# A hybrid decoder step: no drains in the product loops, four banks for the output products, and a sample recurrence on VectorE and ScalarE alone

## The chip, the cores and the metric

One core of one Trainium2 chip runs the whole program. The metric is the device time of one execution in microseconds. The kernel before was run three times: 4519.31 us in the median, 4514.93 to 4529.73 us.

## What is computed

One inference step of one layer of a hybrid decoder, for a prompt of 1024 tokens and for 8 samples of 4 tokens (1056 tokens together, D = 1024, everything float32). Only the token mixer is touched by the change:

```
proj = RMSNorm(h) @ w_in        # gates (3 D) | RWKV-7 (3328) | S5 (1024) | Mamba-2 (z, xBC, dt)
o_r, o_s, o_m = RWKV-7, S5, Mamba-2 of their columns, each projected to D
merged = sig(g_r)*o_r + sig(g_s)*o_s + sig(g_m)*o_m
```

The RWKV-7 state of a sample is, for each of 16 heads, a 64 x 64 matrix S (value x key). For each of the 4 tokens:

```
sa = S a                                        # one number per value row
S  = S diag(w) + sa b^T + v k^T
y  = S r
```

S5 also needs, per channel group, a small Toeplitz kernel made from products of two coefficient tables. After the mixer come cross-attention and a squared-ReLU MLP.

## The kernel before

Every large product is made of three float32r passes: a weight tile is split into a high part (a rounding copy on ScalarE) and a low part (a subtraction on VectorE), and so is the input; TensorE adds hi*hi, hi*lo and lo*hi in PSUM. The 1056 tokens are three column chunks of 352. A block is 128 output columns: 8 contraction tiles x 3 passes x 3 chunks = 72 matmuls.

The order on each engine is written out by hand. Each stage is a set of generators, one per engine and kind of work, that yield a nominal time before they issue something; `weave` merges the generators of an engine by that time. Each engine then works through its own queue in that order, and semaphores join them. A wait therefore holds up all that stands behind it on its engine.

- `Columns` (L143 to L224) makes the input projections in three runs (weights named pz, pa and pb in the trace), 91 blocks, with the S5 and Mamba-2 work woven between. The high copy of the weights of block b (`high`, L188) overwrites a buffer that block b-2 read. TensorE says that it has been read with a drain at the end of each block (L213).
- `S5Input` (L265 to L349) makes the S5 input in two halves, with the same kind of drain, eight times (L347).
- `S5Weights` (L528 to L631) makes the S5 Toeplitz kernels, in 8 rounds. In each, two times eight products (L600), contraction 64, 16 output rows and 128 columns, go to the same 16 partitions of bank 5; the second half waits until ScalarE has moved the first out (L619).
- `Sums` (L1590 to L1763) makes the output products of the branches: 32 jobs of one block each, nominally 13 us apart. Jobs 0 to 7 and 8 to 15 are moved out of PSUM by ScalarE (L1734; the second eight with a sigmoid), jobs 16 to 31 by VectorE (L1754), which also combines every job from 8 on with its gate (L1763). VectorE makes the low part of the weights (L1683) one block ahead, and, at jobs 0, 8, 16 and 24, that of a new input (L1701), in chunks. The chunks go in turn to two PSUM banks, 6 and 7. Each job ends with a drain (L1721), for which `high` (L1677) waits.
- `RwkvSamples` (L1769 to L2053) is woven into the same stage. It builds the six vectors r, w, k, v, a, b of the 32 sample tokens, sends them through DRAM so that a partition holds one sample and head (128 of them), and then runs the recurrence: state, `tmp` and `sw` are tiles of 64 x 64 per partition in `sum_region`. VectorE works in four parts of 128 x 1024: state times a (L1982), its sums (L1986), sa b^T (L1990), plus `sw` (L1996), plus `sw` again (L2003), times r (L2008), its sums (L2012). `sw` is made by GpSimd in one instruction each, first the decayed state (L2050), then v k^T (L2053). VectorE waits for each, and GpSimd waits for VectorE to have read the one before. The first token waits for the vectors (`v_in`) and the state to land.
- `Tails` (L2056 to L2112) transposes the last tokens for some of the outputs, in the same stage, with banks 5 and 0.

The high copy of the sums before is:

```
act.wait_ge(self.loaded[b % 2], 16 * (b // 2 + 1))
if b >= 2:
    act.wait_ge(self.used, b - 1)
self.nc.scalar.activation(self.hi[:, b % 2, :, :], self.raw[:, b % 2, :, :], ACT.Copy).then_inc(self.w_hi, 1)
```

## Time and profile before

| | us |
|---|---|
| median of three runs | 4519.31 |
| the profiled execution, its own time | 4515.67 |
| its span | 4513.9 |
| TensorE busy | 4102.0 |
| VectorE busy | 2517.0 |
| ScalarE busy | 1420.3 |
| GpSimd busy | 222.7 |
| projections with S5 and Mamba-2 | 264 to 1843 |
| branch sums with the sample recurrence | 1860 to 2366 |
| prompt RWKV-7, then attention and MLP | from 2370 on |

Times of the trace count from the start of the span. A row in time gives start, length, engine and line; in brackets is the idle time ahead of it and what ended it. Matmuls overlap, so the distance between two starts says how fast they flow, not the length. Rows of waits give the total, how often and the longest.

### The profile page before, as it was taken

To read this page: it belongs to the slowest core of one execution; us is meant where nothing else is said; L and a number is where in the kernel's file an instruction comes from. 1 tells how busy PE (TensorE), PEld (TensorE's weight loads), DVE (VectorE), ACT (ScalarE), POOL (GpSimd) and SP (SyncE) were. 2 spreads that over 40 slices of the span, in tenths; PEclk is the share of its full clock that TensorE was granted. 3 is DMA by queue.
4 is the path that set the end of the run, shared out by engine and by line. 5 is a ranking of instruction groups with operands and counts; after the bars stand their busy time and mean duration, and the time that the engine had idled before them with its cause. 6 is when DMAs were issued, how large, how long until landed. Compare 5 with 4: busy or idle time off the path is not lost. (4 is left out here: it accounts for less than half of the span.)

```text
span 4513.9 us, 84409 instructions
## 1 busy us (share of the span) xinstructions
PE 4102.0 (91%) x35797; PEld 3747.0 (83%) x35797; DVE 2517.0 (56%) x4994; ACT 1420.3 (31%) x2428; POOL 222.7 (5%) x161
## 2 busy tenths in 40 slices
PE   8789999989989999878886999987998899999998
PEld 4779989989978888777885777776977889999997
DVE  3334646431278885258766877765553255444446
ACT  2112222221167553322103444433531252111112
POOL 0000000000001111022110000000001100000000
PEclk9899999989989999988997999998999999999999
DMA  5222222233355554545541100005222221111112
GB/s 186 77 84 83 89 82 88 69 98 112 104 146 142 159 145 123 155 141 163 176 141 40 32 29 31 32 13 174 92 96 89 74 90 61 47 47 47 39 37 77
DMA packets 374261, 418.68 MB, mean 93 GB/s; under 512 B 49162, under 2 KB 315964, under 8 KB 373020
## 3 DMA queue, kind: packets, MB, share of 16 engines
q1 hardware_dynamic: 361599, 368.01, 26.8%
q0 software_dynamic: 7680, 27.97, 2.1%
q10 hardware_dynamic: 4608, 17.30, 1.0%
q8 instruction: 285, 4.67, 0.4%
q14 instruction: 89, 0.73, 0.1%
HBM read 289.10 MB, written 121.77 MB: 91 GB/s over the span
## 5 line engine op out<-in xcount | busy, mean ns | idle before, releaser
L1718 PE MATMUL bank<-sum_x_hi,sum_w_hi 128*128 128x352 f32 x768 | 262.8, 342 | 95.4 <-DVE sum_x_lo L1701 38.0
L210 PE MATMUL bank<-xn_hi,pz_whi 128*128 128x352 f32 (+1 forms) x984 | 328.2, 334 | 21.0 <-DVE pz_wlo L195 14.9
L210 PE MATMUL bank<-xn_hi,pz_wlo 128*128 128x352 f32 (+1 forms) x984 | 319.7, 325 | 0.0
L210 PE MATMUL bank<-xn_lo,pz_whi 128*128 128x352 f32 (+1 forms) x984 | 318.0, 323 | 0.0
L3071 PE MATMUL bank<-bx_hi,bp_whi 128*128 128x384 f32 (+1 forms) x768 | 273.8, 357 | 29.7 <-DVE bx_lo L3129 18.4
L224 ACT ACTIVATE ring<-bank 128x352 f32<-128x352 f32 (+1 forms) x273 | 125.6, 461 | 536.0 <-PE bank L210 535.6
L210 PE MATMUL bank<-xn_hi,pb_whi 128*128 128x352 f32 x816 | 274.9, 337 | 18.9 <-DVE pb_wlo L195 13.0
L210 PE MATMUL bank<-xn_lo,pb_whi 128*128 128x352 f32 x816 | 266.1, 326 | 0.0
L210 PE MATMUL bank<-xn_hi,pb_wlo 128*128 128x352 f32 x816 | 265.2, 325 | 0.0
L1718 PE MATMUL bank<-sum_x_lo,sum_w_hi 128*128 128x352 f32 x768 | 256.5, 334 | 0.0
L1718 PE MATMUL bank<-sum_x_hi,sum_w_lo 128*128 128x352 f32 x768 | 256.3, 334 | 0.0
L3692 PE MATMUL bank<-bx_hi,bp_whi 128*128 128x384 f32 (+1 forms) x768 | 251.2, 327 | 4.7 <-issue 4.7
L3692 PE MATMUL bank<-ml_hidden_hi,bp_whi 128*128 128x384 f32 (+1 forms) x768 | 254.5, 331 | 0.0
L3071 PE MATMUL bank<-bx_lo,bp_whi 128*128 128x384 f32 (+1 forms) x768 | 253.1, 330 | 0.0
L3071 PE MATMUL bank<-bx_hi,bp_wlo 128*128 128x384 f32 (+1 forms) x768 | 253.0, 329 | 0.0
L3692 PE MATMUL bank<-bx_lo,bp_whi 128*128 128x384 f32 (+1 forms) x768 | 248.6, 324 | 0.0
L3692 PE MATMUL bank<-bx_hi,bp_wlo 128*128 128x384 f32 (+1 forms) x768 | 248.1, 323 | 0.0
L3692 PE MATMUL bank<-ml_hidden_hi,bp_wlo 128*128 128x384 f32 (+1 forms) x768 | 247.8, 323 | 0.0
L3692 PE MATMUL bank<-ml_hidden_lo,bp_whi 128*128 128x384 f32 (+1 forms) x768 | 247.6, 322 | 0.0
L1718 PEld LDWEIGHTS bank<-sum_x_hi,sum_w_hi 128*128 128x128 f32 x768 | 152.6, 199 | 105.6 <-issue 75.9
L3055 DVE TENSOR_TENSOR bp_wlo<-ring,bp_whi 128x512 fp32r<-128x512 f32 x192 | 131.4, 688 | 156.1 <-ACT bp_whi L3049 154.9
L3667 ACT ACTIVATE bp_whi<-ring 128x512 fp32r<-128x512 f32 x152 | 92.0, 627 | 394.4 <-PE bank L3692 391.4
(695 smaller groups left out, 12227.7 us busy)
## 6 DMA issues: line engine op xcount, KB each, us to landing
ring<-in_w_in_dram SPq DMA_DIRECT2D x90, 512.0 KB, 4.9
proj_scratch<-ring SPq DMA_DIRECT2D x66, 528.0 KB, 3.0
m_seg<-acum_scratch SPq DMA_DIRECT2D x32, 512.0 KB, 7.0
ring<-in_mlp_w_dram SPq DMA_DIRECT2D x16, 1024.0 KB, 5.6
ring<-in_mlp_w_dram SPq DMA_DIRECT2D x32, 512.0 KB, 3.5
gates_scratch<-ring SPq DMA_DIRECT2D x24, 528.0 KB, 4.7
merged_scratch<-sum_gate ACTq DMA_DIRECT2D x24, 528.0 KB, 5.7
m_raw<-proj_scratch SPq DMA_DIRECT2D x24, 512.0 KB, 5.5
```

Of the source, the lines that this page charges most:

```text
L210: last = self.nc.tensor.matmul(ps[0:n, 0:m], w[:, q, 0:n], self.pair[x][:, q, t0:t0 + m], start=q == 0 and j == 0, stop=q == KD - 1 and j ...
L224: self.nc.scalar.activation(self.staging[0:n, b % 2, t0:t0 + m], self.banks[e % len(self.banks)][0:n, 0:m], func).then_inc(self.off, 1)
L1718: last = self.nc.tensor.matmul(self.banks[e % n][:, 0:m], w[:, b % 2, q, :], self.pair[x][:, q, t0:t0 + m], start=q == 0 and i == 0, stop= ...
L3055: self.nc.vector.tensor_tensor(self.lo[:, hu % 4, :, :], raw, self.hi[:, hu % 4, :, :], ALU.subtract).then_inc(self.w_lo, 1)
L3071: last = self.nc.tensor.matmul(ps, w[:, hu % 4, q, :], self.pair[x][:, 4 * hf + q, t0:t0 + m], start=hf == 0 and q == 0 and i == 0, stop=h ...
L3667: self.nc.scalar.activation(self.pr.hi[:, hv % 4, :, :], self.raw(hv), ACT.Copy).then_inc(self.w_hi, 1)
L3692: last = self.nc.tensor.matmul(ps, w[:, s, q % 4, :], x[h][:, q, t0:t0 + m], start=q == 0 and j == 0, stop=q == 4 * v.halves - 1 and j == 2)
```

## The change

Five edits. (1) The drains of `Columns` and `Sums` are gone; the high copy waits for the counter of finished chunks instead. (2) In `S5Input` each drain becomes a signal of the matmul itself. (3) The two halves of the S5 kernel products go to partitions 0 to 15 and 64 to 79 of the bank, alternate, and no longer wait for a copy between them. (4) `Sums` gets banks 4 to 7; the samples and `Tails` move to banks 0 to 3, and one sum of the samples also waits for `sig`, whose reader has to be through with bank 1. (5) GpSimd's part of the recurrence is gone: VectorE multiplies the state with w in place, and ScalarE makes v k^T with 64 instructions per token, each a copy of k (128 x 64) scaled by one v per partition.

```diff
@@ Columns.high; Sums.high has the same edit @@
             if b >= 2:
-                act.wait_ge(self.used, b - 1)
+                act.wait_ge(self.product, 3 * (b - 1))
@@ Columns.multiply; Sums.multiply has the same edit @@
                 last.then_inc(self.product, 1)
-            pe.drain().then_inc(self.used, 1)
@@ S5Input.scalar @@
-                if s:
+                if s and q < KD - 1:
                     act.wait_ge(self.freed, q + 1)
+                elif s:
+                    act.wait_ge(self.product, Q5 + 1)
@@ S5Input.tensor @@
-                    if i == Q5 and s == 0:
-                        pe.drain().then_inc(self.freed, 1)
+                    if i == Q5 and s == 0 and q < KD - 1:
+                        last.then_inc(self.freed, 1)
@@ S5 kernel products @@
-            for half in range(2):
-                yield self.at(z, -0.40 + 0.05 * half)
-                pe.wait_ge(self.made_c, z + 1)
-                pe.wait_ge(self.off, 2 * z + 2)
-                if half:
-                    pe.wait_ge(self.kern_off, 2 * z + 1)
-                at = slice(64 * half, 64 * half + 64)
-                for q in range(QP):
-                    for ri in range(2):
-                        last = nc.tensor.matmul(bank[0:GC, q * P:(q + 1) * P], v.bb[at, ri, q0 + q, :],
+            yield self.at(z, -0.40)
+            pe.wait_ge(self.made_c, z + 1)
+            pe.wait_ge(self.off, 2 * z + 2)
+            for q in range(QP):
+                for ri in range(2):
+                    for half in range(2):
+                        at = slice(64 * half, 64 * half + 64)
+                        last = nc.tensor.matmul(bank[64 * half:64 * half + GC, q * P:(q + 1) * P], v.bb[at, ri, q0 + q, :],
...
-                last.then_inc(self.turned, 1)
+            last.then_inc(self.turned, 2)
@@ RwkvSamples.tensor @@
         pe.wait_ge(self.k_sq, 1)
-        nc.tensor.matmul(bank[3][:, 0:W], k.ones64[:, :], flat(T[5]), start=True, stop=True).then_inc(self.k_sum, 1)
+        pe.wait_ge(self.sig, 1)
+        nc.tensor.matmul(bank[1][:, 0:W], k.ones64[:, :], flat(T[5]), start=True, stop=True).then_inc(self.k_sum, 1)
@@ RwkvSamples.scalar @@
+        for t in range(TS):
+            for i in range(64):
+                yield self.RECUR - 2 + t * self.TOKEN + 0.5 * i
+                if t == 0 and i == 0:
+                    act.wait_ge(self.v_in, 16 * NB)
+                if t and i == 0:
+                    act.wait_ge(self.vk_used, t)
+                last = activation(self.sw[:, i, :], self.vt[:, t, RX_K, :], ACT.Copy, scale=self.vt[:, t, RX_V, i:i + 1])
+            last.then_inc(self.vk_made, 1)
@@ RwkvSamples.vector @@
             for i, h in enumerate(part):
                 yield at + 18 + 1.5 * i
-                if i == 0:
-                    dve.wait_ge(self.sw_made, t + 1)
                 dve.drain()
-                last = tt(st[:, h, :], tmp[:, h, :], sw[:, h, :], ALU.add)
-            last.then_inc(self.sw_used, 1)
+                tt(st[:, h, :], st[:, h, :], row(t, RX_W), ALU.mult)
+            for i, h in enumerate(part):
+                yield at + 24 + 1.5 * i
+                dve.drain()
+                tt(st[:, h, :], tmp[:, h, :], st[:, h, :], ALU.add)
@@ RwkvSamples.pool, removed whole @@
-            pool.tensor_tensor(sw, st, row(t, RX_W), ALU.mult).then_inc(self.sw_made, 1)
-            yield at + 24
-            pool.wait_ge(self.sw_used, t + 1)
-            pool.tensor_tensor(sw, vt[:, t, RX_V, :].unsqueeze(2).broadcast_to([P, N, N]), row(t, RX_K), ALU.mult).then_inc(self.vk_made, 1)
@@ branch_sums @@
-        sums = Sums(k, ctx, "sum", pair, inputs, jobs, k.bank[6:8], 13.0)
+        sums = Sums(k, ctx, "sum", pair, inputs, jobs, k.bank[4:8], 13.0)
```

ScalarE's queue where the recurrence starts. L1677 is now L1676, L1693 is L1692, L1734 is L1732, the store L1666 is L1665, and L1910 is a new row of v k^T. Before:

```order
L1734 ACTIVATE sum_gate<-bank7 128x352
L1734 ACTIVATE sum_gate<-bank6 128x352
L1666 DMA merged_scratch<-sum_gate 128x1056
L1677 ACTIVATE sum_w_hi<-ring 128x1024
L1693 ACTIVATE sum_x_hi<-ring 128x8x352
L1734 ACTIVATE sum_gate<-bank7 128x352
L1693 ACTIVATE sum_x_hi<-ring 128x8x352
```

And now:

```order
L1732 ACTIVATE sum_gate<-bank7 128x352
L1910 ACTIVATE sum_region<-sum_region 128x64 x3
L1732 ACTIVATE sum_gate<-bank4 128x352
L1910 ACTIVATE sum_region<-sum_region 128x64 x2
L1665 DMA merged_scratch<-sum_gate 128x1056
L1910 ACTIVATE sum_region<-sum_region 128x64 x2
L1676 ACTIVATE sum_w_hi<-ring 128x1024
L1910 ACTIVATE sum_region<-sum_region 128x64 x5
L1692 ACTIVATE sum_x_hi<-ring 128x8x352
L1732 ACTIVATE sum_gate<-bank5 128x352
L1910 ACTIVATE sum_region<-sum_region 128x64 x8
L1692 ACTIVATE sum_x_hi<-ring 128x8x352
```

The first of the new rows, with its wait for `v_in`, stands ahead of the last copy out of job 6, of all of job 7's, and of the high parts of job 8's weights and input.

VectorE's queue in the middle of the first token. Before:

```order
L1996 TENSOR_TENSOR sum_region<-sum_region 128x1024 x4
L1683 TENSOR_TENSOR sum_w_lo<-ring,sum_w_hi 128x1024
L1763 TENSOR_TENSOR sum_gate<-sum_gate,sum_prev 128x1056
L2003 TENSOR_TENSOR sum_region<-sum_region 128x1024 x4
L1683 TENSOR_TENSOR sum_w_lo<-ring,sum_w_hi 128x1024
```

And now, with L1682 for L1683 and L1761 for L1763:

```order
L2002 TENSOR_TENSOR sum_region<-sum_region 128x1024 x4
L2006 TENSOR_TENSOR sum_region<-sum_region 128x1024 x4
L1682 TENSOR_TENSOR sum_w_lo<-ring,sum_w_hi 128x1024
L1761 TENSOR_TENSOR sum_gate<-sum_gate,sum_prev 128x1056
L2012 TENSOR_TENSOR sum_region<-sum_region 128x1024 x4
L1682 TENSOR_TENSOR sum_w_lo<-ring,sum_w_hi 128x1024
```

The decay (L2002) is four instructions more ahead of the same low part of the weights; the rest keeps its place.

## Rows read from the trace of the kernel before

**Rows 1.** The page: busy time, share of the span and count of instructions, by engine.

```profile
PE 4102.0 (91%) x35797; PEld 3747.0 (83%) x35797; DVE 2517.0 (56%) x4994; ACT 1420.3 (31%) x2428; POOL 222.7 (5%) x161
```

**Rows 2.** Stretches: length, busy time of five engines, granted clock, DMA share, GB/s.

```profile
264.00:927.00 663.00, 640.99 (x4782) 594.19 (x4782) 338.98 (x1058) 166.94 (x292) 0.00 (x0) 1.00 0.27 82
1975.00:2366.00 391.00, 314.26 (x1793) 304.11 (x1791) 300.50 (x221) 60.84 (x64) 71.78 (x18) 0.90 0.47 153
```

**Rows 3.** TensorE in time (start, length): end of a projection block.

```profile
603.16 0.32 PE L210 MATMUL bank<-xn_hi,pz_wlo 128*128 128x352 f32 x1
603.74 0.40 PE L210 MATMUL bank<-xn_hi,pz_whi 128*128 128x352 f32 x1 [0.26 <-issue]
```

**Rows 4.** TensorE in time: between two column chunks of one block.

```profile
1880.45 0.32 PE L1718 MATMUL bank<-sum_x_hi,sum_w_lo 128*128 128x352 f32 x1
1880.61 0.32 PE L1718 MATMUL bank<-sum_x_hi,sum_w_hi 128*128 128x352 f32 x1
```

**Rows 5.** Drains in TensorE's queue: count, ns min/median/max, first and last start.

```profile
L213 PEldq DRAIN  x91: 3062/3088/3125, 274.1 to 1839.0; - x91
L1721 PEldq DRAIN  x32: 3050/3050/4558, 1873.4 to 2358.8; - x32
L347 PEldq DRAIN  x8: 843/860/4010, 184.4 to 194.2; - x8
```

**Rows 6.** TensorE in time: row-tiled products, then the S5 kernel products.

```profile
648.02 0.71 PE L739 MATMUL bank<-s_ca,s_H 64*128 64x128 f32 x8 [0.26 <-issue]
...
658.79 1.90 PE L600 MATMUL bank<-s_ca,s_bb 64*16 64x128 f32 x16 [0.78 <-ACT s_wb L613]
```

**Rows 7.** TensorE's waits from 1975 to 2366 us: total, times, longest.

```profile
PE bank L1718 <- DVE sum_prev L1754: 29.0, 7, 12.6
PE bank L1718 <- DVE sum_x_lo L1701: 17.4, 1, 17.4
PE bank L1718 <- ACT sum_gate L1734: 13.2, 6, 3.1
PE bank L1718 <- DVE sum_gate L1754: 10.2, 3, 9.7
```

**Rows 8.** GpSimd in time, one of its eight products.

```profile
2036.67 9.95 POOL L2050 TENSOR_TENSOR sum_region<-sum_region 128x4096 f32<-128x4096 f32 x1 [6.41 <-DVE sum_region L2003]
```

**Rows 9.** VectorE in time: one row beside that product, one free of it.

```profile
2037.82 9.93 DVE L1763 TENSOR_TENSOR sum_gate<-sum_gate,sum_prev 128x1056 f32<-128x1056 f32 x1
...
2059.36 1.26 DVE L1763 TENSOR_TENSOR sum_gate<-sum_gate,sum_prev 128x1056 f32<-128x1056 f32 x1
```

**Rows 10.** GpSimd's products by group: busy, mean ns, idle before.

```profile
L2050 POOL TENSOR_TENSOR sum_region<-sum_region 128x4096 f32<-128x4096 f32 x4 | 37.5, 9364 | 47.4 <-DVE sum_region L2003 35.1 <-DMA sum_region<-vec_scratch 12.3
L2053 POOL TENSOR_TENSOR sum_region<-sum_region 128x4096 f32<-128x4096 f32 x4 | 29.2, 7294 | 207.9 <-DVE sum_region L1996 207.9
```

**Rows 11.** VectorE by group, 1981 to 2325 us.

```profile
L1763 DVE TENSOR_TENSOR sum_gate<-sum_gate,sum_prev 128x1056 f32<-128x1056 f32 x20 | 47.4, 2371 | 1.7
L2008 DVE TENSOR_TENSOR sum_region<-sum_region 128x1024 f32<-128x1024 f32 x16 | 36.4, 2278 | 1.3
L1982 DVE TENSOR_TENSOR sum_region<-sum_region 128x1024 f32<-128x1024 f32 x16 | 28.2, 1765 | 23.6 <-DMA sum_region<-vec_scratch 22.1 <-issue 0.4
L1996 DVE TENSOR_TENSOR sum_region<-sum_region 128x1024 f32<-128x1024 f32 x16 | 19.6, 1226 | 1.3
```

**Rows 12.** In time around the recurrence's start: VectorE, then TensorE.

```profile
1981.49 11.16 DVE L1982 TENSOR_TENSOR sum_region<-sum_region 128x1024 f32<-128x1024 f32 x2 [22.05 <-DMA sum_region<-vec_scratch]
...
1998.21 0.63 PE L1718 MATMUL bank<-sum_x_hi,sum_w_hi 128*128 128x352 f32 x1 [17.43 <-DVE sum_x_lo L1701]
1998.64 0.49 PE L1718 MATMUL bank<-sum_x_lo,sum_w_hi 128*128 128x352 f32 x1
1998.94 0.49 PE L1718 MATMUL bank<-sum_x_hi,sum_w_lo 128*128 128x352 f32 x1
```

**Rows 13.** ScalarE by group: the nearest to the new rows.

```profile
L1443 ACT ACTIVATE r_U<-bank 128x64 f32<-128x64 f32 x128 | 28.5, 222 | 98.5 <-PE bank L1086 98.5
```

More of the change, by code:

```diff
@@ L618, in scalar @@
                     act.wait_ge(self.placed[1 - s], 16 * Q5 * ((z + 1) // 2))
-                activation(v.kern[:, half:ZG:2, :], bank[0:GC, :].rearrange("p (q n) -> p q n", q=QP), ACT.Copy).then_inc(self.kern_off, 1)
+                activation(v.kern[:, half:ZG:2, :], bank[64 * half:64 * half + GC, :].rearrange("p (q n) -> p q n", q=QP), ACT.Copy).then_inc(self.kern_off, 1)
     def sync(self, sp, used):
@@ L1598, in __init__ @@
         self.loaded, self.stored, self.gate_in, self.prev_in, self.x_in = two("loaded"), three("stored"), three("gate_in"), three("prev_in"), two("x_in")
-        self.w_hi, self.w_lo, self.used, self.product, self.done, self.x_hi, self.x_lo, self.sig = (
-            S("w_hi"), S("w_lo"), S("used"), S("product"), S("done"), S("x_hi"), S("x_lo"), S("sig"))
+        self.w_hi, self.w_lo, self.product, self.done, self.x_hi, self.x_lo, self.sig = (
+            S("w_hi"), S("w_lo"), S("product"), S("done"), S("x_hi"), S("x_lo"), S("sig"))
         self.off = [S(f"off{i}") for i in range(len(banks))]
@@ L1675, in high @@
             if b >= 2:
-                act.wait_ge(self.used, b - 1)
+                act.wait_ge(self.product, 3 * (b - 1))
             self.nc.scalar.activation(self.hi[:, b % 2, :, :], self.raw[:, b % 2, :, :], ACT.Copy).then_inc(self.w_hi, 1)
@@ L1720, in multiply @@
                 last.then_inc(self.product, 1)
-            pe.drain().then_inc(self.used, 1)
     def evacuate_scalar(self, act):
@@ L1851, in tensor @@
         pe.wait_ge(self.k_sq, 1)
-        nc.tensor.matmul(bank[3][:, 0:W], k.ones64[:, :], flat(T[5]), start=True, stop=True).then_inc(self.k_sum, 1)
+        pe.wait_ge(self.sig, 1)
+        nc.tensor.matmul(bank[1][:, 0:W], k.ones64[:, :], flat(T[5]), start=True, stop=True).then_inc(self.k_sum, 1)
         yield 44
         pe.wait_ge(self.bon, 1)
-        nc.tensor.matmul(bank[4][:, 0:W], k.ones64[:, :], flat(T[6]), start=True, stop=True).then_inc(self.bon_sum, 1)
+        nc.tensor.matmul(bank[2][:, 0:W], k.ones64[:, :], flat(T[6]), start=True, stop=True).then_inc(self.bon_sum, 1)
         six = [self.pm[:, 0:8, :], T[0], T[7], self.pm[:, 16:24, :], T[9], T[8]]
@@ L1864, in tensor @@
             for q in range(4):
-                last = nc.tensor.transpose(bank[(5, 0)[n % 2]][0:NS, q * P:(q + 1) * P], six[n // 2][:, 4 * (n % 2) + q, :], k.ident[:, :])
+                last = nc.tensor.transpose(bank[(3, 0)[n % 2]][0:NS, q * P:(q + 1) * P], six[n // 2][:, 4 * (n % 2) + q, :], k.ident[:, :])
             last.then_inc(self.tok_turned, 1)
@@ L1880, in tensor @@
         pe.wait_ge(self.squared, 1)
-        nc.tensor.matmul(bank[4][:, 0:W], k.ones64[:, :], self.f0, start=True, stop=True).then_inc(self.varsum, 1)
+        nc.tensor.matmul(bank[0][:, 0:W], k.ones64[:, :], self.f0, start=True, stop=True).then_inc(self.varsum, 1)
     def scalar(self, act):
@@ L1910, in scalar @@
         act.wait_ge(self.varsum, 1)
-        activation(self.f1, k.bank[4][:, 0:W], ACT.Ln, bias=k.eps[:, 2:3], scale=1.0 / 64)
+        activation(self.f1, k.bank[0][:, 0:W], ACT.Ln, bias=k.eps[:, 2:3], scale=1.0 / 64)
         act.drain()
@@ L1960, in vector @@
         dve.wait_ge(self.bon_sum, 1)
-        tt(self.bonus, bank[4][:, 0:W].rearrange("p (j t) -> p j t", t=NS), val, ALU.mult).then_inc(self.bonused, 1)
+        tt(self.bonus, bank[2][:, 0:W].rearrange("p (j t) -> p j t", t=NS), val, ALU.mult).then_inc(self.bonused, 1)
         for n in range(12):
@@ L1966, in vector @@
                 dve.wait_ge(self.tails.out, 16 * (3 + NB))
-            nc.vector.tensor_copy(self.tok[:, (n // 2) * D + (n % 2) * 512:(n // 2) * D + (n % 2 + 1) * 512], bank[(5, 0)[n % 2]][0:NS, :]).then_inc(self.tok_off, 1)
+            nc.vector.tensor_copy(self.tok[:, (n // 2) * D + (n % 2) * 512:(n // 2) * D + (n % 2 + 1) * 512], bank[(3, 0)[n % 2]][0:NS, :]).then_inc(self.tok_off, 1)
         N = 64
@@ L2003, in vector @@
                 last = tt(st[:, h, :], st[:, h, :], sw[:, h, :], ALU.add)
-            last.then_inc(self.st_made, 1)
+            last.then_inc(self.vk_used, 1)
             for i, h in enumerate(part):
@@ L2036, in vector @@
         tt(y, y, bank[2][:, 0:W], ALU.mult).then_inc(self.gated, 1)
-    def pool(self, pool):
-        N = 64
-        st, sw, vt = self.st, self.sw, self.vt
-        row = lambda t, a: vt[:, t, a, :].unsqueeze(1).broadcast_to([P, N, N])
-        for t in range(TS):
-            at = self.RECUR + t * self.TOKEN
-            yield at
-            if t == 0:
-                pool.wait_ge(self.v_in, 16 * NB)
-                pool.wait_ge(self.s_in, 16)
-            else:
-                pool.wait_ge(self.st_made, t)
-            pool.tensor_tensor(sw, st, row(t, RX_W), ALU.mult).then_inc(self.sw_made, 1)
-            yield at + 24
-            pool.wait_ge(self.sw_used, t + 1)
-            pool.tensor_tensor(sw, vt[:, t, RX_V, :].unsqueeze(2).broadcast_to([P, N, N]), row(t, RX_K), ALU.mult).then_inc(self.vk_made, 1)
 class Tails:
@@ L2101, in tensor @@
             for q in range(n):
-                last = self.nc.tensor.transpose(self.k.bank[(5, 0)[i % 2]][0:TAIL, q * P:(q + 1) * P], self.tile[:, a + q, :], self.k.ident[:, :])
+                last = self.nc.tensor.transpose(self.k.bank[(3, 0)[i % 2]][0:TAIL, q * P:(q + 1) * P], self.tile[:, a + q, :], self.k.ident[:, :])
             last.then_inc(self.turned, 1)
@@ L2111, in vector @@
             c = a if a < RT else a - RT
-            self.nc.vector.tensor_copy(self.rows[:, c * P:(c + n) * P], self.k.bank[(5, 0)[i % 2]][0:TAIL, 0:n * P]).then_inc(self.copied, 1)
+            self.nc.vector.tensor_copy(self.rows[:, c * P:(c + n) * P], self.k.bank[(3, 0)[i % 2]][0:TAIL, 0:n * P]).then_inc(self.copied, 1)
 def branch_sums(k, v):
@@ L2140, in _ @@
             def _(pool):
-                weave(later(samples.sync(pool), late), later(samples.pool(pool), late), tails.sync(pool))
+                weave(later(samples.sync(pool), late), tails.sync(pool))
             @block.tensor
```

8 lines of the change are left out of this document (4 added, 4 removed).

## The prediction

> **What bounds it now.** The page first: TensorE is busy 91% of the span, GpSimd 5% [rows 1]. Then the stretches [rows 2]: in the first projection run TensorE works 641 of 663 us at full clock, so what ends there is TensorE's own stream; in the part of the branch sums where the recurrence runs it works 314 of 391 us at a mean granted clock of 0.90, and VectorE is busy for 300.5. So two things are to be read: what breaks TensorE's stream where it is full, and whom it waits for in the sums.
>
> TensorE in time answers the first. Two matmuls of 352 columns start 0.16 us apart, also across a chunk that has a satisfied wait [rows 4]; across a block's end the distance is 0.58 us, with 0.26 us idle that nothing but "issue" ends [rows 3]. What stands there alone is the drain, of which there are 91, 32 and 8 [rows 5]. A drain row is 3.1 us long, but that is the time the queue runs ahead of the array; the array loses 0.58 - 0.16 = 0.42 us.
>
> The waits answer the second. From 1975 us on TensorE waits 29.0 + 10.2 us for VectorE to empty a bank, 13.2 for ScalarE to do so and 17.4 for the new input's low part [rows 7]. Behind them stands GpSimd: while one of its products runs for 9.95 us, a VectorE instruction that takes 1.26 us alone takes 9.93 [rows 8, 9]. It is not slowed by a share, it stands still until GpSimd is done. GpSimd's eight products sum to 66.7 us [rows 10], and on three lines of VectorE the excess over the undisturbed row is 22 (L1763: 47.4 - 20 x 1.26), 17 (L2008) and 9 us (L1982, both against 19.6) [rows 9, 11]: 48 us found, at most 66.7.
>
> **Part by part.**
>
> *Drains of the projections.* 91 x 0.42 would be 38 us. Where the next work is a small product of S5 or Mamba-2 the array would have paused a little anyway, so I count 0.34 on average: 31 us. Bounds: nothing, if another engine is just behind TensorE everywhere, and 38. I stay near the upper end, because 641 of 663 us busy leaves no room for another gate [rows 2].
>
> *Drains of S5Input.* Eight, at most 0.42 each [rows 3, 5]; I take 2 us of 0 to 3. The signals of single matmuls that replace seven of them cost nothing: matmuls with a signal stand at each chunk's end and the next starts 0.16 us later [rows 4].
>
> *S5 kernels.* Sixteen products take 1.90 us one after the other; eight of the same contraction and columns, on two row groups in turn, take 0.71 us with their fill [rows 6]. Without the last product's own length (some 0.27 of it) that is 0.10 us against 0.055 us each. 16 x 0.05 x 8 rounds is 6 us, and one entry fewer in some rounds another: 7 us. Bounds 0 (the halves do not overlap) and 9.
>
> *Branch sums up to the recurrence.* Eight drains, 3 us. The moved banks and the wait on `sig` cost nothing here: the product that has it stands in a queue of matmuls, and VectorE's two additions ahead of `sig` are 128 x 256; a microsecond at most.
>
> *The recurrence's part of the sums.* The stretch of 391 us holds 1793 matmuls [rows 2]; at 0.16 us [rows 4] that is 287. Waits are 69.8 [rows 7], 24 drains 10, and the remaining 24 I put at slow restarts (20) and the ends (4): after a pause the starts are 0.30 us apart instead of 0.16 (0.49 us long instead of 0.32) [rows 4, 12], which is half clock, 1.2 GHz instead of 2.4. Now the same sum after the change:
> - The first pause, 17.4 us. VectorE waits 22 us for the vectors, then GpSimd blocks it: the first two parts take 11.16 us instead of 2.5 [rows 9, 11, 12]. That goes, but ScalarE now waits for the same vectors, with the high parts of job 8 behind it, so these 5 us of work come later. TensorE has banks for the four chunks that ScalarE leaves, so it gets as far as before. I keep 11 us.
> - The waits on VectorE and ScalarE for banks, 52.4 us. Long ones come when GpSimd blocks VectorE, up to 12.6 at a time; with four banks a block of 10 us would hardly show. But VectorE also makes the low weights only one block ahead, and that is not deeper now. VectorE gets back 48 to 66.7 us and is given 16 instructions of 1.226 us, 20 us [rows 11]; from 300.5 its load is then 254 to 272 us beside TensorE's 287. It is not the bound, but within a token it has more to do than TensorE and falls behind by some 10 us; that shows at jobs 16 and 24, where a new input needs three low parts too. I keep 22 us.
> - Drains 0, slow restarts 11, as there are about half as many pauses.
> So 391 becomes 287 + 33 + 11 + 4 = 335, 56 less.
> - ScalarE gets 256 rows of 128 x 64. The nearest row, the same size out of PSUM, takes 222 ns [rows 13]: 57 us on an engine busy for 60.8 of 391 [rows 2]. Upper end: twice that row, since these read SBUF and take their scale from a tile, 114 us. Either is covered by its 330 idle us; from where it is not, see the third rival.
>
> The Trainium skill (page "GPSIMD Engine Reference", section 8, "Key points") speaks only of contention with VectorE instructions that have two SBUF inputs; read as a fair share, VectorE would get back half of GpSimd's 66.7 us, 33, and be given 20: the sums would then go by the first rival, 4447 us. The trace has the whole of a product's length on the row beside, so I take the whole.
>
> The sum: 31 + 2 + 7 + 3 + 56 = 99 us. The profiled execution took 4515.67 us (span 4513.9 and 1.8 around it), 3.6 below the median of 4519.31. The forecast for the median is 4519.3 - 99 = 4420 us.
>
> **Rivals.**
> 1. *VectorE's queue becomes the gate of the sums.* For: its load, 254 to 272 us in a stage that would last 335, in strict order, each wait for a product putting it behind; the low weights one block ahead. Against: the idle it had ahead of the low inputs and gates. The waits then stay near 60 instead of 33: 27 us less gain, 4447 us. Chance 0.17.
> 2. *The projections don't follow.* VectorE, ScalarE or the loads of S5 and Mamba-2 are just behind TensorE, and a block's 0.42 us turns into a wait for them. For: ScalarE and VectorE wait for each other there too. Against: the 22 us in all that TensorE is not busy [rows 2]. 25 of the 31 us go: 4445 us. Chance 0.1.
> 3. *Slower than before: ScalarE's rows hold the queue.* Some 26 rows fall into a block of 11.5 us (72 x 0.16), beside a high copy and three moves out of PSUM. From about 0.35 us a row ScalarE is later than TensorE in those blocks, and its queue holds both the high weights and the banks. To lose the 99 us and 13 more, the excess over 0.35 us times 256 has to be 112 us: 0.79 us a row, three and a half times the nearest row [rows 13]. The Trainium skill warns against small tiles on ScalarE and VectorE (page "Advanced Engine Details and Errata", section "The Read-Write Bubble") and asks for 512 elements or more; that is the direction, not the size. At 0.85 us the time is 4420 + 256 x 0.5 = 4548 us. Chance 0.03.
> 4. *More than forecast.* VectorE keeps up, and of the waits only the first pause stays: 20 us more, and the projections give all of 38: 4393 us. Chance 0.08.
> 5. *The halves of the S5 kernels don't overlap*, so that this edit doesn't do what it says: 4427 us, inside the forecast's own spread. It is part of the forecast's chance, 0.62.
>
> **The numbers.** Forecast 0.62. The range goes from 4392 us, the fourth rival, to 4458, beyond the first two with a little of both: about 1 in 10 is left out above and less below. A measurement of this kernel can tell 0.3%, 13.6 us, from no change. Faster by more: 0.95. Within it: 0.02, for a sum of rivals 1, 2 and a weak form of 3. Slower: 0.03, rival 3.
>
> **What would show it.** Projections: blocks' ends 0.16 us apart, TensorE's busy share of that stretch above 98%, pz, pa and pb together some 31 us shorter. S5 kernels: 16 products in about 1 us. Sums: no VectorE row of L1761 or the low weights beyond 1.3 us; TensorE's waits from the recurrence on 25 to 40 us, the largest one the new input at job 8; the stage some 59 us shorter; rows of v k^T 0.22 to 0.32 us and no wait of VectorE for them. Wrong would be: VectorE or ScalarE without idle time and TensorE waiting for low weights in most blocks; or a stretch that is not touched (after 2370 us) that changes its length by more than 5 us.

## The result, and the profile after

| | before | after |
|---|---|---|
| median, us | 4523.39 (4 runs, 4514.93 to 4529.73) | 4397.77 (4 runs, 4397.24 to 4403.45) |
| ratio | | 0.9726, 95% interval 0.9714 to 0.9738 |
| span of the profiled execution | 4513.9 | 4395.8 |

Forecast were 4420 us in a range of 4392 to 4458. The time is in the range, 22 us below the forecast. Stage by stage, each from its first to its last matmul, the two profiled executions differ like this (us):

| | before | after | gain |
|---|---|---|---|
| S5 input | 111.2 | 109.8 | 1.4 |
| pz, 41 blocks | 656.8 | 623.5 | 33.3 |
| pa, 16 blocks | 310.2 | 308.9 | 1.3 |
| pb, 34 blocks | 577.2 | 569.7 | 7.5 |
| sums, up to the end of job 7 | 120.1 | 116.5 | 3.5 |
| sums, the recurrence's part | 381.0 | 314.7 | 66.3 |
| prompt RWKV-7 | 660.5 | 660.2 | 0.3 |

That is 113.6 of 118.1 us; the rest is between stages, 3 us of it behind the sums, where nothing was changed. The medians are 7.5 us further apart than the profiled executions, which the section on the hardware comes back to. Times of stages below are of one profiled execution of each kernel, measured in this way; where only the sums are named, it is both of their parts together (501.1 before, 431.3 after).

The busy times answer to [rows 1], the two stretches to [rows 2]. The page of the changed kernel:

```profile
PE 4044.1 (92%) x35797; PEld 3722.4 (85%) x35797; DVE 2481.2 (56%) x5010; ACT 1482.6 (34%) x2684; POOL 156.8 (4%) x153
```

And its stretches (length, then busy time of TensorE, its weight loads, VectorE, ScalarE, GpSimd, granted clock, DMA share, GB/s):

```profile
261.00:889.00 628.00, 618.07 (x4782) 585.23 (x4782) 338.84 (x1059) 168.65 (x292) 0.00 (x0) 1.00 0.28 86
1932.00:2249.00 317.00, 288.44 (x1759) 284.41 (x1757) 263.68 (x237) 123.72 (x320) 5.11 (x10) 0.97 0.57 186
```

The same 4782 matmuls of the first projection take 628 us instead of 663. In the recurrence's part VectorE is busy for 263.7 us, inside the 254 to 272 of the forecast, and the granted clock is 0.97 where it was 0.90.

TensorE in time (start, length, engine, line) at a block's end, against [rows 3]: blocks follow each other 0.17 us apart, where it was 0.58. Below it the S5 kernel products, against [rows 6]:

```profile
581.85 0.32 PE L210 MATMUL bank<-xn_hi,pz_wlo 128*128 128x352 f32 x1
582.02 0.32 PE L210 MATMUL bank<-xn_hi,pz_whi 128*128 128x352 f32 x1
...
635.82 1.92 PE L599 MATMUL bank<-s_ca,s_bb 64*16 64x128 f32 x32 [0.78 <-ACT s_wb L612]
```

Here the forecast is caught out. The visit holds 32 rows in 1.92 us; [rows 6] has 16 in 1.90. The trace has 256 rows on this line in both kernels, 32 a round, though the program issues 16 products a round: one product makes two rows. So the 16 rows of [rows 6] were one half of a round and not both.

TensorE's waits in the recurrence's part (in total, times, longest), against [rows 7]:

```profile
PE bank L1717 <- DVE sum_x_lo L1700: 24.9, 7, 11.4
PE bank L1717 <- issue: 1.4, 1, 1.4
PE bank L1717 <- DVE sum_w_lo L1682: 1.2, 2, 0.9
PE bank L1880 <- ACT sum_region L1915: 1.0, 1, 1.0
```

No wait for an emptied bank is left, of 52.4 us; nearly all of the 28.5 is for the low part of a new input, with the first one, at job 8, the longest, as forecast. VectorE by group (busy, mean ns, idle time before), against [rows 9, 11], and the new rows of ScalarE, against [rows 13]:

```profile
L1761 DVE TENSOR_TENSOR sum_gate<-sum_gate,sum_prev 128x1056 f32<-128x1056 f32 x24 | 30.2, 1258 | 2.8 <-issue 0.9
L2002 DVE TENSOR_TENSOR sum_region<-sum_region 128x1024 f32<-128x1024 f32 x16 | 19.6, 1226 | 1.3
L2012 DVE TENSOR_TENSOR sum_region<-sum_region 128x1024 f32<-128x1024 f32 x16 | 19.6, 1225 | 1.3
L2017 DVE TENSOR_TENSOR sum_region<-sum_region 128x1024 f32<-128x1024 f32 x16 | 19.6, 1225 | 1.3
...
L1910 ACT ACTIVATE sum_region<-sum_region 128x64 f32<-128x64 f32 x256 | 64.9, 335 | 53.6 <-DVE sum_gate L1761 36.9 <-DMA sum_region<-vec_scratch 16.0
```

The gate's sum is at 1.26 us in the mean where it was 2.37, the products with r (now L2017) at 1.23 where they were 2.28. L2012, which adds v k^T, has 1.3 us idle ahead of 16 instructions: VectorE does not wait for ScalarE's rows.

### The profile page after: what moved, and what is told of

Its sections match the earlier page's. It is cut to its first block and busy times, and to the rows that moved or that the text cites. A ratio compares the mean times of both kernels' runs of the same rounds, so it can differ in the third digit from the quotient of the medians.

```text
span 4395.8 us, 84548 instructions
## 1 busy us (share of the span) xinstructions
PE 4044.1 (92%) x35797; PEld 3722.4 (85%) x35797; DVE 2481.2 (56%) x5010; ACT 1482.6 (34%) x2684; POOL 156.8 (4%) x153
## 5 line engine op out<-in xcount | busy, mean ns | idle before, releaser
L210 PEld LDWEIGHTS bank<-xn_hi,pz_whi 128*128 128x128 f32 (+1 forms) x984 | 184.0, 187 | 20.1 <-DVE pz_wlo L195 15.1
```

The lines of the kernel that those rows point to most:

```text
L210: last = self.nc.tensor.matmul(ps[0:n, 0:m], w[:, q, 0:n], self.pair[x][:, q, t0:t0 + m], start=q == 0 and j == 0, stop=q == KD - 1 and j ...
```

## The experiments

The first four kernels put one part of the change into the kernel before; their ratios are against 14 runs of it (median 4525.24 us). The next four, each one edit away from the changed kernel, have 7 runs of the kernel before beside them (median 4521.77), and the last two another 7 (4528.09). The two in between, with idle work on GpSimd, were run once each.

### Without the drains (edits 1 and 2)

```diff
-            pe.drain().then_inc(self.used, 1)
-                act.wait_ge(self.used, b - 1)
+                act.wait_ge(self.product, 3 * (b - 1))
```

> Only the drains are taken out of the kernel before (projections, S5 input, sums); the rest is as it was. Theory: each costs TensorE 0.27 to 0.42 us and nothing else, so pz gets 17 us shorter, pa 1 to 5, pb 7 to 12, the S5 input 2, the sums 8 to 12 (some of theirs stand ahead of waits): 35 to 45 us in all, about 4480 us. Rival: the drains also paced the engines, and most of what the full change gained in pz came from them: pz 25 us or more shorter, over 50 us in all. A second rival, that the other engines are just behind: under 20 us.

Measured: 4480.2 us, ratio 0.9905 (0.9885 to 0.9924). pz loses 15.3 us (0.37 a block), pa 2.4, pb 6.4 (0.19 a block), the S5 input 2.4, the sums 4.9. In pb 34 x 0.37 would be 12.6 us; of the 6.2 that lack, 2.7 are seen as waits for `m_seg`, which Mamba-2 makes on VectorE. TensorE's waits in pb, of the kernel before, of this one and of the changed one:

```profile
PE bank L2739 <- DVE m_seg L2824: 4.3, 2, 2.4
```
```profile
PE bank L2739 <- DVE m_seg L2824: 7.0, 5, 2.4
```
```profile
PE bank L2731 <- DVE m_seg L2816: 10.9, 7, 2.4
```

So a drain costs TensorE some 0.4 us where nothing else is just behind it, and on average half of that where the engines of Mamba-2 are. In the sums 8 to 12 us were expected and 4.9 came, 2.7 of them in the recurrence's part: there most of what a drain costs is taken up by the waits behind it. The median fell by 45 us, but these stages hold only 31.4 us of the 38.2 between the two profiled executions; 6 us more lie behind the sums, where nothing was changed.

### The halves of the S5 kernels (edit 3)

```diff
-                at = slice(64 * half, 64 * half + 64)
-                        last = nc.tensor.matmul(bank[0:GC, q * P:(q + 1) * P], v.bb[at, ri, q0 + q, :],
+                    for half in range(2):
+                        last = nc.tensor.matmul(bank[64 * half:64 * half + GC, q * P:(q + 1) * P], v.bb[at, ri, q0 + q, :],
```

> Only the two halves of the S5 kernel products are put side by side. Theory: my term was sized with a half's rows for both halves, so that it is twice as large: L600's products take some 15 us less of TensorE's time and pz gets 14 to 17 us shorter; the whole about 4507 us. Rival: the products overlap as forecast, 7 us, and the rest of pz's gain belongs to the drains: pz 7 us shorter.

Measured: 4510.28 us, ratio 0.9964 (0.9951 to 0.9977). pz loses 15.8 us, eight rounds of almost 2. TensorE in time, one round of this kernel:

```profile
649.22 1.92 PE L598 MATMUL bank<-s_ca,s_bb 64*16 64x128 f32 x32 [0.78 <-ACT s_wb L611]
```

Against 16 rows in 1.90 us in [rows 6], the rows follow each other twice as fast: the halves overlap in full. The fifth rival falls.

### Four banks (edit 4)

```diff
-        sums = Sums(k, ctx, "sum", pair, inputs, jobs, k.bank[6:8], 13.0)
+        sums = Sums(k, ctx, "sum", pair, inputs, jobs, k.bank[4:8], 13.0)
```

> Only the banks: sums on four banks, samples and tails moved; GpSimd stays in the recurrence. Theory: GpSimd's stalls of VectorE (7 to 10 us each) are longer than two banks (7.6 us of TensorE's work) and about as long as four, less what low weights need; so the banks alone already hide a good part: TensorE's waits in the sums fall from 70 to about 45 us and the stage gets 20 to 30 us shorter. Rival A: the banks are nothing by themselves since the low weights are only one block ahead: under 8 us. Rival B: the banks are all of the stage's gain: 60 us or more.

Measured: 4503.32 us, ratio 0.9949 (0.9928 to 0.997), the sums 501.1 to 483.0, 18.1 less. TensorE's waits in the recurrence's part:

```profile
PE bank L1718 <- DVE sum_x_lo L1701: 30.6, 8, 17.3
PE bank L1718 <- DVE sum_w_lo L1683: 13.8, 4, 6.5
PE bank L1718 <- DVE sum_gate L1754: 5.9, 1, 5.9
PE bank L1718 <- DVE sum_prev L1754: 4.1, 1, 4.1
```

That is just under the 20 to 30 us expected. Of the 52.4 us of waits for banks 10.4 are left, and VectorE's block is waited for one step on: 13.8 us for the low weights, which stood at nothing, and 13 more for low inputs. Deeper banks cover only the one thing that VectorE makes late.

### The recurrence without GpSimd (edit 5)

```diff
-            pool.tensor_tensor(sw, st, row(t, RX_W), ALU.mult).then_inc(self.sw_made, 1)
+                tt(st[:, h, :], st[:, h, :], row(t, RX_W), ALU.mult)
-            pool.tensor_tensor(sw, vt[:, t, RX_V, :].unsqueeze(2).broadcast_to([P, N, N]), row(t, RX_K), ALU.mult).then_inc(self.vk_made, 1)
+                last = activation(self.sw[:, i, :], self.vt[:, t, RX_K, :], ACT.Copy, scale=self.vt[:, t, RX_V, i:i + 1])
```

> Only the recurrence without GpSimd; two banks, drains and serial halves stay. Theory: VectorE is never held, so no VectorE row of the combining products is longer than 1.3 us, and TensorE's waits in the sums fall from 70 to 35 to 45 us; the stage gets 35 to 50 us shorter. Rival A: without the banks VectorE's extra 20 us of work and ScalarE's rows show as bank waits: under 20 us. Rival B: all of the stage's gain comes from here: 60 us or more.

Measured: 4484.78 us, ratio 0.9913 (0.9887 to 0.994), the sums 462.9 us, 38.2 less: the largest part of the change there. The waits of TensorE:

```profile
PE bank L1718 <- ACT sum_gate L1734: 18.9, 6, 8.1
PE bank L1718 <- DVE sum_prev L1754: 14.9, 8, 4.3
PE bank L1718 <- DVE sum_gate L1754: 3.7, 3, 3.1
```

Those for VectorE to empty a bank are 18.6 us instead of 39.2, and none is over 4.3 (12.6 before). ScalarE's are 5.7 us more, with one of 8.1: its rows stand ahead of copies out of a bank.

In ratios the four parts give 0.0095 + 0.0036 + 0.0051 + 0.0087 = 0.0269, the change 0.0274; their intervals leave some 0.004 open, 18 us, so this doesn't show whether the whole is more than its parts. The sums' stage tells more: the parts give 4.9 + 18.1 + 38.2 = 61.2 us and the change 69.8. The 8.6 us between them lie ahead of job 8's first matmul. From it to the end of the sums the parts give 2.6 + 21.5 + 35.7 = 59.8 us and the change 60.3 (363.3 us in the kernel before, 303.0 in the changed one). The next experiment asks what stands ahead of job 8.

### Two banks in the changed kernel

```diff
-        sums = Sums(k, ctx, "sum", pair, inputs, jobs, k.bank[4:8], 13.0)
+        sums = Sums(k, ctx, "sum", pair, inputs, jobs, k.bank[6:8], 13.0)
```

> The changed kernel, but its sums go back to two banks (6 and 7). Theory: with GpSimd gone VectorE is late by at most a few microseconds at a time, mostly within a token, so the two extra banks are worth less than the 18 us that they gave beside GpSimd: the sums stage gets 8 to 15 us longer (431 to about 443 us). Rival: the gains of banks and of a free VectorE need each other (the four edits alone give 61 us in this stage, together 70), so that the stage gets 20 to 30 us longer. If the banks were nothing now: under 4 us.

Measured: 4421.34 us, ratio 0.9778 (0.9763 to 0.9793); the sums 454.3 us, 23.0 more. The rival has the size right: four banks are worth 23.0 us beside a free VectorE and 18.1 beside a blocked one. Its reason, that the two gains need each other, isn't shown: from job 8's first matmul on four banks are worth 18.7 us here and 21.5 beside a blocked VectorE, so in that part they are worth a little less, as the theory had it, though more than its 8 to 15. What is new lies ahead of job 8. There ScalarE's new rows wait for the vectors, with copies out of a bank behind them. Two banks leave TensorE standing behind that, and the longest wait, 9.6 us, is this one. It makes 4.3 of the 23.0 us, so half of the 8.6; the other half is no more than the spread of that part from kernel to kernel (last section):

```profile
PE bank L1717 <- ACT sum_gate L1732: 18.8, 6, 9.6
PE bank L1717 <- DVE sum_prev L1752: 13.3, 6, 3.8
PE bank L1717 <- DVE sum_gate L1752: 4.3, 5, 3.1
```

Only some 8 of the 23 us are more idle time of TensorE. For the rest it is busy longer, 414 us instead of 400 on the same matmuls: the granted clock is 0.91 up to the end of job 7 and 0.94 behind it, where the changed kernel has 0.97 in both. More and shorter waits came with a lower clock here; what ties the one to the other wasn't tried.

### v k^T on GpSimd again

```diff
-                last = activation(self.sw[:, i, :], self.vt[:, t, RX_K, :], ACT.Copy, scale=self.vt[:, t, RX_V, i:i + 1])
+            pool.tensor_tensor(sw, vt[:, t, RX_V, :].unsqueeze(2).broadcast_to([P, N, N]), row(t, RX_K), ALU.mult).then_inc(self.vk_made, 1)
```

> The changed kernel, but v k^T of each token is one GpSimd product again, issued as soon as its buffer is free, so that nobody waits for it; ScalarE has no rows. Theory: each of the four products (7 to 8 us) holds VectorE for its whole length, a VectorE row of 7 us or more stands beside each, and with VectorE nearly full in the tokens this can't be caught up: the stage gets 12 to 25 us longer. Rival: what hurt before was waiting for GpSimd, not its work; then the stage is as long as with ScalarE's rows or shorter, within 4 us.

Measured: 4421.43 us, ratio 0.9778 (0.9761 to 0.9795); the sums 460.9 us, 29.6 more, above the expected 12 to 25. Four products of GpSimd suffice for that, and VectorE has no idle time in which it waits for them. What they do is seen where one of them runs (GpSimd, then VectorE, in time):

```profile
1986.21 7.98 POOL L2049 TENSOR_TENSOR sum_region<-sum_region 128x4096 f32<-128x4096 f32 x1 [44.89 <-DVE sum_region L2003]
```
```profile
1987.35 7.95 DVE L1761 TENSOR_TENSOR sum_gate<-sum_gate,sum_prev 128x1056 f32<-128x1056 f32 x1
```

Of GpSimd's 30.1 us VectorE loses 26.8: L1761 35.6 us instead of the 28.9 of 23 undisturbed rows, and the two recurrence products beside it 32.8 and 26.5 instead of 19.6.

### Half rows on ScalarE

```diff
-                last = activation(self.sw[:, i, :], self.vt[:, t, RX_K, :], ACT.Copy, scale=self.vt[:, t, RX_V, i:i + 1])
+                for c in (slice(0, 32), slice(32, 64)):
+                    last = activation(self.sw[:, i, c], self.vt[:, t, RX_K, c], ACT.Copy, scale=self.vt[:, t, RX_V, i:i + 1])
```

> The changed kernel with each row of v k^T in two instructions of 32 columns: 512 instead of 256 on ScalarE. Theory: ScalarE has room; some 50 us more work on it, no wait of VectorE for it, and the stage changes by less than 4 us. Rival (the forecast's third in small): the queue of ScalarE is near its limit in blocks with rows, high weights and bank copies come late, and the stage gets 15 us or more longer.

Measured: 4405.41 us, ratio 0.9744 (0.9729 to 0.9758); the sums 440.5 us, 9.2 more, between theory and rival. ScalarE by group:

```profile
L1911 ACT ACTIVATE sum_region<-sum_region 128x32 f32<-128x32 f32 x512 | 112.2, 308 | 30.8 <-DVE sum_gate L1761 15.7 <-DMA sum_region<-vec_scratch 14.4
```

Of the 9.2 us, 5.6 are in the recurrence's part; the other 3.6 stand ahead of it, where TensorE waits no longer than before and is busy for longer at a lower granted clock, as in other kernels that have no half rows (last section). So 47.3 us more on an engine busy for 124 of 317 cost 5 to 6 us. The rows are not free, then: VectorE waits for ScalarE's high parts for 12.9 + 12.7 us instead of 8.9 + 10.0. A row costs by its number (0.31 us for 32 elements, 0.34 for 64), hardly by its size.

### The recurrence later

```diff
-    RECUR, TOKEN, FINISH = 80, 76, 396
+    RECUR, TOKEN, FINISH = 94, 72, 396
-        yield self.RECUR - 16
+        yield 64
```

The transfers of the vectors keep their place, and so does the end; only what waits for them stands 14 nominal us further back, behind the high parts of job 8.

> The changed kernel with the recurrence placed 14 nominal us later and its tokens 72 instead of 76 apart, the loads of its vectors where they were. ScalarE and VectorE meet the wait for the vectors after the high and low parts of job 8's input. Theory: the pause at job 8 (11.4 us, and 1.2 and 2.8 after it) shrinks to what a new input costs elsewhere (3 to 6 us), and the tokens still end in time: 8 to 12 us less in the stage and in all, about 4387 us. Rival: VectorE, nearly full in a token, becomes fuller with 72, and gives it back as waits for low parts and banks: within 4 us of the changed kernel or slower.

Measured: 4386.98 us, ratio 0.9704 (0.9689 to 0.9718), 10.8 us below the changed kernel; the sums 418.4 us, 12.9 less. **This beats both kernels.** ScalarE and VectorE waited for the vectors with the parts of job 8's input behind them; that pause of TensorE is 3.85 us now, where it was 11.38. The first line is of the changed kernel, the second of this one:

```profile
1943.74 0.63 PE L1717 MATMUL bank<-sum_x_hi,sum_w_hi 128*128 128x352 f32 x1 [11.38 <-DVE sum_x_lo L1700]
```
```profile
1944.71 0.66 PE L1717 MATMUL bank<-sum_x_hi,sum_w_hi 128*128 128x352 f32 x1 [3.85 <-DVE sum_x_lo L1700]
```

### What it is in GpSimd's work that stops VectorE

Two kernels give GpSimd work that nobody reads, at the places of the old products: 14 instructions of 128 x 256, twice a token, copies in the first and products of two inputs in the second.

```diff
+            for _ in range(14):
+                pool.tensor_copy(junk[:, 1, :], junk[:, 0, :])
+                pool.drain()
```

> The changed kernel, with GpSimd doing idle work of its own in the recurrence again: per token twice 14 instructions of 128 x 256, here copies with one input, with a drain between them, about where the two products of 128 x 4096 stood. Nothing reads what they make. The question is what in GpSimd's work stops VectorE. Theory: it is the two-input product, whose reads hold what VectorE's two-input instructions need; a copy with one input leaves VectorE alone or nearly so: no row of the gate's sum (128 x 1056) over 1.6 us, the four recurrence groups within 10% of the changed kernel's means, and the sums' stage 431 us as it is, at most 436. Rival: any GpSimd instruction stops VectorE: rows of the gate's sum of 2 to 5 us, and the stage 10 to 30 us longer, as with the two-input form.

> The same with products of two inputs of 128 x 256 in place of the copies. Theory (a GpSimd instruction with two inputs holds a VectorE instruction with two inputs for its whole length, and only while it runs): a piece is about a sixteenth of a 128 x 4096 product, some 0.6 us, and VectorE gets in between pieces. So no row of VectorE waits for 9.9 us any more; rows of the gate's sum beside pieces take 1.26 plus one or two pieces, 1.9 to 3 us, and the stage is 5 to 20 us longer than the changed kernel's 431. Rival 1: it holds VectorE from the first piece to the last of a group, as before: rows of 7 to 10 us. Rival 2: the stop before came from the broadcast inputs or the large size and not from the form: then nothing grows, and rows stay at 1.26 us.

Measured, one run each: 4400.6 us with copies, the sums 440.8; 4414.25 us with products, the sums 446.7. By group in the kernel with products, GpSimd first, then VectorE:

```profile
L2067 POOL TENSOR_TENSOR junk<-junk 128x256 f32<-128x256 f32 x56 | 80.4, 1435 | 114.3 <-DVE sum_region L1998 106.9
```
```profile
L2003 DVE TENSOR_TENSOR sum_region<-sum_region 128x1024 f32<-128x1024 f32 x16 | 23.7, 1482 | 1.3
L1994 DVE TENSOR_REDUCE sum_region<-sum_region 128x16 f32<-128x1024 f32 x16 | 19.5, 1220 | 1.3
```

GpSimd is busy for 140 us in all, twice what it was before the change, and VectorE loses 17.7 where it lost 48 or more: no row is over 1.68 us in the recurrence or 1.51 at the gate. VectorE's sums, with one input, lose nothing. The expected rows of 1.9 to 3 us at the gate did not come, the expected 5 to 20 us of the stage did (15.4). With copies a recurrence row takes 1.30 at most in the mean (L2003), and VectorE loses 5 us in all. The first rival of both falls. The limit of 436 us for copies was missed: TensorE is busy for 7.6 us more there on the same matmuls, at a lower granted clock, and the whole run is only 2.8 us above the changed kernel.

### v k^T on GpSimd in pieces

If VectorE stands still only for the length of one GpSimd instruction, v k^T can go back if it is cut up: 16 pieces of four value rows. The first kernel has a drain between pieces, the second doesn't.

```diff
+            for i in range(0, N, 4):
+                last = pool.tensor_tensor(sw[:, i:i + 4, :], vt[:, t, RX_V, i:i + 4].unsqueeze(2).broadcast_to([P, 4, N]), vt[:, t, RX_K, :].unsqueeze(1).broadcast_to([P, 4, N]), ALU.mult)
+                if i < N - 4:
+                    pool.drain()
```

> v k^T back on GpSimd, but in 16 pieces of 4 value rows (128 x 256) each token with a drain between them, in place of one product of 128 x 4096; ScalarE has no rows. In one product this cost 29.6 us of the sums' stage against the rows on ScalarE (461 against 431 us). Theory: VectorE stands still for a whole GpSimd instruction that has two inputs, and gets in between two of them, so short ones only share: with 64 pieces where the study with idle work had 112 and lost 15 us of the stage, the stage should be 3 to 10 us longer than with ScalarE's rows, 434 to 441 us, no VectorE row beside them over 1.8 us where it takes 1.26 alone, and the time 4400 to 4409 us. GpSimd needs 64 x 1.07 to 1.44, 68 to 92 us in place of some 29. Rival: GpSimd's work costs VectorE the same time in any cutting, and the stage stays at 455 us or more, the time at 4418 or more. Second rival: freed of its 256 rows ScalarE brings the high parts sooner, the stage gets shorter than 431 and the time goes below 4397.

> The same 16 pieces without the drains between them, so that GpSimd issues them back to back. If VectorE gets in at the boundary of an instruction, it is as with the drains or a few us better, since GpSimd is through sooner: stage 434 to 441 us. If it gets in only in the pause that a drain makes, VectorE stands still for the whole string of 16, some 7 to 10 us as before, and the stage is at 455 us or more, the time at 4418 or more.

Measured: with drains 4402.92 us, ratio 0.9732 (0.9709 to 0.9756), the sums 436.6; without them 4410.34, ratio 0.975 (0.9722 to 0.9777), the sums 438.0. Both stages are where the theory put them. The kernel without drains, GpSimd and VectorE in time:

```profile
1982.76 16.04 POOL L2050 TENSOR_TENSOR sum_region<-sum_region 128x256 f32<-128x256 f32 x16 [27.40 <-DVE sum_region L2003]
```
```profile
1983.91 1.49 DVE L1761 TENSOR_TENSOR sum_gate<-sum_gate,sum_prev 128x1056 f32<-128x1056 f32 x1
1985.50 6.12 DVE L2008 TENSOR_TENSOR sum_region<-sum_region 128x1024 f32<-128x1024 f32 x4
1991.69 5.10 DVE L2012 TENSOR_REDUCE sum_region<-sum_region 128x16 f32<-128x1024 f32 x4
```

The same row at the same place of the program, beside the same work: 7.95 us in one piece, 1.49 in sixteen. The two engines take turns. Two pieces of this string, the first beside VectorE's products with two inputs, the second beside its sums with one:

```profile
1985.84 1.59 POOL L2050 TENSOR_TENSOR sum_region<-sum_region 128x256 f32<-128x256 f32 x1
1992.63 0.61 POOL L2050 TENSOR_TENSOR sum_region<-sum_region 128x256 f32<-128x256 f32 x1
```

Beside the products there is one piece to each row of VectorE; a piece takes 1 us longer than beside the sums, and the row 0.25 us longer than alone. VectorE loses 6.7 us in place of 26.8, though GpSimd is busy for 66.0 in place of 30.1, and the stage costs 7 us over the changed kernel in place of 29.6. A drain between pieces isn't needed for that. The times of the two kernels don't overlap (4401.1 to 4405.8 with drains, 4409.5 to 4413.4 without), but of the 8.6 us between their profiled executions only 1.4 are in the sums, and 7.2 behind them, where the two programs are the same. So this doesn't tell whether the drains help. Neither beats ScalarE's rows, and the second rival, a gain from a freed ScalarE, falls.

## Why the prediction was right, and where it was off

**Drains of the projections: 31 us forecast, 24 shown** (15.3 + 2.4 + 6.4, alone). In pz the price of 0.42 us held almost whole, 0.37. The step of this term that failed is "641 of 663 us busy leaves no room for another gate": that was the stretch of pz, and it was carried over to pb, where `m_seg` and other work of Mamba-2 is just behind. The second rival named this mechanism; it holds in pb in part (2.7 us of such waits are seen), and not in pz.

**S5Input: 2 us forecast**, 2.4 alone, 1.4 in the change. **Up to the recurrence: 3**, measured 3.5.

**S5 kernels: 7 us forecast, 15.8 shown, outside the bound of 9.** The term was mis-sized because "sixteen products take 1.90 us one after the other" took the rows for products. It was one half, eight products of two rows each; the other half came in a later visit. So 32 rows at 0.12 us became 32 at 0.06: 32 x 0.06 x 8 rounds = 15 us. The count in [rows 6] could have been held against the loops, which issue eight products a half. This term gave 8.8 us more than forecast and the drains 7 less, and that the two errors cancel is luck; pz, pa and pb together came out at 42.1 us against 38.

**The recurrence's part: 56 us forecast, 66.3 measured.** The mechanism was the right one: GpSimd's products on the row beside. Part by part: of the first pause 11 us were to stay, and 11.4 did. Of the waits for banks and parts 22 were to stay, and 17 did (28.5 - 11.4), none of them for a bank. So the waits fell by 41.3 us and not by 36.8. For drains, slow restarts and the ends 10 + 9 + 0 us were forecast, and 66.3 - 41.3 = 25 are left for them. How they divide isn't shown: the drains alone gave 2.7 us in this part, and in the kernel before only 16 of the 24 show as idle time.

```profile
PE bank L1718 <- issue: 4.2, 16, 0.3
```

The rest is TensorE busy for 287 us instead of 307 on the same matmuls, with the granted clock up from 0.90 to 0.97. So the surplus of 10.3 us is 4.5 of waits and some 6 of drains and restarts, both in the direction that fewer pauses give.

The loss of VectorE was counted a little too low. A fourth line is slowed, the low weights, in the same list as [rows 11]:

```profile
L1683 DVE TENSOR_TENSOR sum_w_lo<-ring,sum_w_hi 128x1024 fp32r<-128x1024 f32 x23 | 34.5, 1498 | 11.7 <-ACT sum_w_hi L1677 11.7
```

Against 1.22 us a row that is 6.5 us more, so 54 of GpSimd's 66.7 us are found and not 48. The term didn't hang on it, since its load of 254 to 272 us allowed for both.

What wasn't foreseen is that ScalarE's wait for the vectors would block banks too. Four banks cover that. The 8.6 us that the parts lack lie there, about half of them shown by the kernel with two banks.

**The rivals.** VectorE's queue didn't become the gate: 28.5 us of waits and not 60. The rule of the Trainium skill (page "GPSIMD Engine Reference", section 8, "Key points") names contention with instructions that have two SBUF inputs. The traces agree on which ones: sums with one input stay at 1.22 us beside the short pieces, the only GpSimd work that they ever stood beside. Beside a long product ran an addition that has one of its inputs in PSUM; it took 0.52 us there as elsewhere. GpSimd, then VectorE, in the kernel before:

```profile
2190.95 7.07 POOL L2053 TENSOR_TENSOR sum_region<-sum_region 128x4096 f32<-128x4096 f32 x1 [58.15 <-DVE sum_region L1996]
2194.01 0.52 DVE L1754 TENSOR_TENSOR sum_prev<-bank,sum_prev 128x352 f32<-128x352 f32 x1 [2.70 <-PE bank L1718]
```

The traces disagree with the fair share that was read into it: 26.8 of 30.1 us are lost to long products, 6.7 of 66.0 to short ones. ScalarE's rows took 0.335 us as the trace has them, a little over the 0.32 expected and under the 0.35 from which they were to hold the queue; one after another they start 0.24 us apart (eight in 2.01 us). Doubling their number cost 5 to 6 us in the recurrence's part, so the third rival's way exists; its size was far. The Trainium skill (page "Advanced Engine Details and Errata", section "The Read-Write Bubble") warns of small tiles there, and 0.31 us for 32 elements against 0.34 for 64 agrees with it.

The stretch that nobody touched, from the last matmul of the sums to the end, went from 2152.0 to 2148.7 us. That is within the 5 us of the forecast's sign, but the two kernels with pieces differ by 7.2 there without an edit, so the sign is weaker than it looks.

## What to carry to other kernels

In these traces a long GpSimd instruction with two inputs stops VectorE's instructions of two SBUF inputs until it is over, so its own length is what it costs and not its share: take it away, give the work to an idle ScalarE, or cut it into pieces that are shorter than VectorE's own instructions, which alone took 23 of 30 us off. More banks cover only the emptying of banks; look what the same late engine also makes (low parts of weights and inputs here) before counting on them, and put a wait for a far transfer behind the work that the main engine needs next, which alone gave 11 us here. Before rows of a trace are priced as instructions, count them against the program's loops.

## What the runs showed of the hardware

- *A row of the trace is not always an instruction.* A float32 product of 64 x 16 weights on 128 columns leaves two rows; 16 products a round left 32. On two row groups in turn they start 0.06 us apart, on the same one 0.12.
- *Much of the spread of this kernel goes with TensorE's clock.* The slowest and the fastest run of the kernel before, 4530.88 and 4506.99 us, have a mean granted clock of 0.952 and 0.959. In no kernel with one edit alone other than the drains is the pa stage touched, and still it took 310 us in the kernel before and 321 in two of them, on the same work and with the same 6.2 us in which TensorE is not busy. The kernel before, then the one with four banks:

```profile
933.00:1243.00 310.00, 303.77 (x2023) 291.92 (x2022) 83.09 (x193) 68.87 (x112) 0.93 (x1) 0.93 0.37 104
```
```profile
933.00:1254.00 321.00, 314.77 (x2024) 302.69 (x2023) 83.14 (x194) 68.76 (x112) 0.87 (x1) 0.90 0.35 100
```

  The granted clock is 0.93 and 0.90: more of the stage at 1.2 GHz instead of 2.4. The profiled execution of the kernel before lies 7.7 us under its median and that of the changed one 0.3, which is why the two medians are 125.6 us apart and the two profiles 118.1. The sums vary too: up to the end of job 7 the changed kernel and the seven other kernels with four banks and no GpSimd product of the decay have TensorE idle for 3 to 5 us, and that part took 116.5 to 120.2 us. So a difference of under 4 us in the sums is not a reading. What makes a spell of half clock start in pa was not found, and not tried.
- *GpSimd is slowed too.* Pieces of 128 x 256 took 1.07 to 1.44 us in the mean with two inputs and 0.82 to 1.12 with one, where a sixteenth of a long product is 0.46 to 0.59 [rows 10]. In the kernel with pieces and no drains it is 1.59 us beside VectorE's products of two inputs, 0.61 beside its sums of one, and 3.46 beside a low part of the input that itself takes 3.2 to 3.5.
